# Norm boundaries of an four-layer fp32 kernel: wide products ended bank by bank, two weight splits moved to GpSimd

## What is computed

```python
# first block, twice
hs = hs + rms_norm(mixer(rms_norm(hs, w0)), w1)
hs = hs + rms_norm(conv_ffn(rms_norm(hs, w2)), w3)
# second block, twice
x = layer_norm(ALPHA * x + mixer(x), g_mix, b_mix)
x = layer_norm(ALPHA * x + swiglu(x), g_ffn, b_ffn)
```

## Time and profile before

| | |
|---|---|
| median of 3 runs | 1444.98 us (1444.98 to 1446.88) |
| span of the profiled execution | 1443.1 us |
| PE busy | 1423.5 us, 99% |
| DVE, ACT, Pool busy | 1013.4, 779.4, 294.0 us |
| chain that ended last | PE 81%, DVE 12%, issue 3%, ACT 3% |
| granted PE clock | 0.999 of full over the span |

### The profile page before, as it was taken

One profiled execution on the slowest core, in us unless ns is written; L12 is line 12 of the kernel. 1 busy time (PEld: TensorE's weight loads), 2 busy tenths in 40 slices (PEclk: granted clock), 3 DMA queues, 4 the chain that ended last, 5 costly groups with the idle time before them and its releaser, 6 DMA issues.

```text
span 1443.1 us, 31771 instructions
## 1 busy us (share of the span) xinstructions
PE 1423.5 (99%) x11333; PEld 1363.9 (95%) x11333; DVE 1013.4 (70%) x1701; ACT 779.4 (54%) x1399; POOL 294.0 (20%) x348
## 2 busy tenths in 40 slices
PE   9999999999999999999999999999999999999997
PEld 8999888899999999999999999999999989999986
DVE  7884957659876477569888477587664687776645
ACT  6556324556655366466565356464453567654542
POOL 3804002103444000002544000013330012033310
PEclk9999999999999999999999999999999999999999
DMA  7551231244655535344666544546556433565552
GB/s 256 177 175 47 88 101 47 93 142 160 190 175 175 175 119 189 103 146 128 193 189 189 182 134 152 164 146 200 183 168 204 152 116 118 163 217 186 183 180 91
DMA packets 60996, 223.57 MB, mean 155 GB/s; under 512 B 6768, under 2 KB 6896, under 8 KB 60528
## 3 DMA queue, kind: packets, MB, share of 16 engines
q1 hardware_dynamic: 60624, 220.17, 48.1%
q10 hardware_dynamic: 288, 2.23, 0.4%
HBM read 221.32 MB, written 1.05 MB: 154 GB/s over the span
## 4 chain that ended last, share of the span: by engine, by line
PE 81%; DVE 12%; issue 3%; ACT 3%; DVEq 1%; ACTq 0%; POOL 0%; POOLq 0%
PE bank L440 20%; PE bank L441 20%; PE bank L442 20%; DVE wlo L415 3%; PE bank L461 2%; PE bank L1168 2%; PE bank L462 1%; PE bank L468 1%; DVE bank L947 1%; PE bank L3284 1%; PE bank L3285 1%; PE bank L3287 1%; ACT cv L831 1%; DVE cv L839 1%; DVE work L1782 1%
## 5 line engine op out<-in xcount | busy, mean ns | idle before, releaser
L415 DVE TENSOR_TENSOR wlo<-raw,whi 128x1024 fp32r<-128x1024 f32 x397 | 501.4, 1268 | 249.3 <-ACT whi L410 248.8
L410 ACT ACTIVATE whi<-raw 128x1024 fp32r<-128x1024 f32 x397 | 415.1, 1056 | 288.6 <-PE bank L442 240.6
L440 PE MATMUL bank<-xs,whi 128*128 128x258 f32 (+2 forms) x1984 | 569.2, 287 | 0.0
L441 PE MATMUL bank<-xs,whi 128*128 128x258 f32 (+2 forms) x1984 | 563.9, 284 | 0.0
L442 PE MATMUL bank<-xs,wlo 128*128 128x258 f32 (+2 forms) x1984 | 561.6, 283 | 0.0
L440 PEld LDWEIGHTS bank<-xs,whi 128*128 128x128 f32 x1984 | 374.2, 189 | 3.0 <-issue 1.6
L442 PEld LDWEIGHTS bank<-xs,wlo 128*128 128x128 f32 x1984 | 375.0, 189 | 0.0
L441 PEld LDWEIGHTS bank<-xs,whi 128*128 128x128 f32 x1984 | 374.3, 189 | 0.6 <-issue 0.2
L440 PE MATMUL bank<-hf,whi 128*128 (+3 forms) x848 | 241.3, 285 | 2.0 <-DVE cv L839 0.8
L441 PE MATMUL bank<-hf,whi 128*128 (+3 forms) x848 | 240.3, 283 | 0.0
L442 PE MATMUL bank<-hf,wlo 128*128 (+3 forms) x848 | 240.2, 283 | 0.0
(11 more groups left out here) (516 smaller groups left out, 1671.8 us busy)
## 6 DMA issues: line engine op xcount, KB each, us to landing
raw<-stream SPq DMA_DIRECT2D x412, 512.0 KB, 3.7
con<-consts SPq DMA_DIRECT2D x1, 1284.5 KB, 10.5
big<-mla ACTq DMA_DIRECT2D x1, 1152.0 KB, 7.8
hs_sb<-hs SPq DMA_DIRECT2D x2, 544.0 KB, 4.2
work<-last ACTq DMA_DIRECT2D x1, 1024.0 KB, 9.1
y_out<-work SPq DMA_DIRECT2D x4, 256.0 KB, 2.0
par<-params SPq DMA_DIRECT2D x1, 420.0 KB, 7.9
par<-params SPq DMA_DIRECT2D x1, 224.0 KB, 4.8
```

The lines of the kernel that those rows point to most:

```text
L410: nc.scalar.activation(whi[:, s, :], raw[:, s, :], ACT.Copy).then_inc(hi_split, 1)
L415: nc.vector.tensor_tensor(wlo[:, s, :], raw[:, s, :], whi[:, s, :].bitcast(F32), ALU.subtract).then_inc(block_split, 1)
L440: nc.tensor.matmul(out_, whi[:, slot, w], hi, start=start, stop=False)
L441: nc.tensor.matmul(out_, whi[:, slot, w], lo, start=False, stop=False)
```

## The change

1. `pe_wide`: the last two rows are no longer done one after the other. `last_two` goes through the eight banks and does both rows in each, so that bank m is complete every 6 matmuls; both blocks are used up only at bank 7.
2. Sums: DVE adds the squares of tiles 0 to 6 (`LAST_SUM = 6`; in the layer norms the first seven, `YSUM = 7`), each addition followed by that bank's `scaled`; PE makes two accumulations instead of four (six in the layer norms). All eight banks are now copied into `y`.
3. Splits: `split_lo_pool` gives the low parts of B1 and B2 to Pool. ACT makes B1's high part behind the table load, B2's behind the squares (in the layer norms behind the beta column, before the first `c{m}`). DVE waits for Pool's two before it splits B3. The queue of Pool's other work stands behind these splits.
4. The wave: block B2 starts with its high part alone (`hi_split`), and its low-part matmuls are done from step `LATE = 5` on, five of the eight at the end.
5. DVE's order in the wave: `lo(m-2)` between `y{m}` and `h{m}` (behind `c{m}` in the layer norms) instead of `lo(m-1)` behind them.

```diff
+    def split_lo_pool(pool, phase):
+        for n in (used_after(phase) + 1, used_after(phase) + 2):
+            s = n % SLOTS
+            pool.wait_ge(hi_split, splits(n))
+            pool.wait_ge(block_split, splits(n - 1))
+            nc.gpsimd.tensor_tensor(wlo[:, s, :], raw[:, s, :], whi[:, s, :].bitcast(F32), ALU.subtract).then_inc(block_split, 1)
+        pool.wait_ge(block_split, splits(used_after(phase) + 2))
...
+            if k == LATE:
+                pe.wait_ge(block_split, splits(b0 + AHEAD - 1))
+            for c in range(k - LATE, k - LATE + 1) if k < KC else range(KC - LATE, KC):
+                if c >= 0:
+                    last = mm(rhs_out(g0 + AHEAD - 1, phase), wlo[:, (b0 + AHEAD - 1) % SLOTS, c * P:(c + 1) * P], xs[:, c, T], start=False, stop=(c == KC - 1))
...
+        def last_two():
+            for m in range(8):
+                for k in (n - 2, n - 1):
...
+                    last = three(rhs_out(g0 + m, phase), (b0 + k) % SLOTS, m, hf[:, half[k], T], hf[:, half[n + k], T], False, k == n - 1)
+                    if m == 7:
+                        last.then_inc(block_used, 1)
...
-        sums_pe(pe, name, post_src(name), g, ((5, True, False), (6, False, False), (0, False, False), (7, False, True)), T1, POST_FIRST[name])
+        sums_pe(pe, name, post_src(name), g, ((0, True, False), (7, False, True)), T1, POST_FIRST[name])
...
-        for m in range(1, IN_BANK):
+        for m in range(1, KC):
+            if m <= LAST_SUM:
+                dve.wait_ge(*S("norm", "act").at(f"{name}_{m}"))
+                if m > 1:
+                    dve.wait_ge(*v.at(f"{name}_sum{m - 1}"))
+                nc.vector.tensor_tensor(sq[:, 0, lo:T1], sq[:, 0, lo:T1], sq[:, m, lo:T1], ALU.add).then_inc(*v.mark(f"{name}_sum{m}"))
             scaled(m)
-        split()
...
+        nc.vector.tensor_tensor(y[:, m, t], y[:, m, t], rs[:, 1, t], ALU.mult).then_inc(*v.mark(f"{name}_y{m}"))
+        if m > 1:
+            lo(m - 2)
         dve.wait_ge(*v.at(f"{name}_y{m}"))
...
-    YSUM = 3
+    YSUM = 7
...
-        sums_pe(pe, name + "m", ln_src(name), g, ((0, True, False), (3, False, False), (4, False, False), (5, False, False),
-                                                  (6, False, False), (7, False, True)), T2)
+        sums_pe(pe, name + "m", ln_src(name), g, ((0, True, False), (7, False, True)), T2)
...
-            act.wait_ge(block_used, used_after(PHASE_BEFORE[phase]) - 1)
+            act.wait_ge(block_used, FIRST_BLOCK[PHASE_BEFORE[phase]])
             nc.scalar.activation(xs[:, 0:KC, T2:TB], alone(beta, 2), ACT.Copy).then_inc(*a_.mark(f"{name}_bhi"))
+            split_hi(act, used_after(PHASE_BEFORE[phase]) + AHEAD - 1)
...
         if phase:
+            dve.wait_ge(block_split, splits(fourth(phase) - 1))
             split_lo(dve, fourth(phase))
...
-        split_all(act, split_hi, "down0", 1, COUNT["down0"] - 2)
+        split_all(act, split_hi, "down0", 1, COUNT["down0"] - 3)
         nc.scalar.preload_act_table_set(LN_EXP)
+        split_hi(act, used_after("down0") + 1)
         post_act(act, "post1", G["post1"], "down0")
...
-        split_all(dve, split_lo, "down0", 1, COUNT["down0"] - 2)
-        post_dve(dve, "post1", G["post1"], 3, lambda: split_lo(dve, used_after("down0") + AHEAD - 1))
+        split_all(dve, split_lo, "down0", 1, COUNT["down0"] - 3)
+        post_dve(dve, "post1", G["post1"], 3)
```

More of the change, by code:

```diff
@@ L457, in pe_tiles @@
                     o, s = rhs_out(g0 + j, phase), (b0 + j) % SLOTS
+                    behind_split = j == AHEAD - 1
                     if k == 0:
-                        pe.wait_ge(block_split, splits(b0 + j))
+                        pe.wait_ge(*((hi_split if behind_split else block_split), splits(b0 + j)))
                         pe.wait_ge(bank_free, g0 + j + 1)
                     mm(o, whi[:, s, w], xs[:, k, T], start=(k == 0), stop=False)
-                    mm(o, wlo[:, s, w], xs[:, k, T], start=False, stop=False)
+                    if not behind_split:
+                        mm(o, wlo[:, s, w], xs[:, k, T], start=False, stop=False)
             if k:
@@ L538, in rows @@
                     bank_ready(pe, (g0 + m) % 8)
-                last = three(rhs_out(g0 + m, phase), (b0 + k) % SLOTS, m, hf[:, half[at] if i is None else at, T], hf[:, half[lo] if i is None else lo, T], k == 0, k == n - 1)
-                if i is None and k == n - 1 and m < 7:
-                    last.then_inc(*S("wide", "pe").mark(f"{phase}_m{m}"))
+                last = three(rhs_out(g0 + m, phase), (b0 + k) % SLOTS, m, hf[:, half[at] if i is None else at, T], hf[:, half[lo] if i is None else lo, T], k == 0, False)
             if done:
                 last.then_inc(block_used, 1)
+        def last_two():
+            for m in range(8):
+                for k in (n - 2, n - 1):
+                    if m == 0:
+                        pe.wait_ge(block_split, splits(b0 + k))
+                        ready(pe, k, None)
+                    last = three(rhs_out(g0 + m, phase), (b0 + k) % SLOTS, m, hf[:, half[k], T], hf[:, half[n + k], T], False, k == n - 1)
+                    if m == 7:
+                        last.then_inc(block_used, 1)
+                    elif k == n - 1:
+                        last.then_inc(*S("wide", "pe").mark(f"{phase}_m{m}"))
         if n == 22:
@@ L549, in pe_wide @@
                     rows(k, i)
-            for k in range(17, 22):
+            for k in range(17, 20):
                 rows(k)
+            last_two()
         else:
@@ L558, in pe_wide @@
                         between(pe, k)
-            for k in range(together, n):
+            for k in range(together, n - 2):
                 rows(k)
+            last_two()
     def pe_sum(pe, name, g, src, T):
@@ L706, in post_act, with post_dve @@
         nc.scalar.activation(rs[:, 1, lo:T1], rs[:, 1, lo:T1], ACT.Exp, scale=-0.5).then_inc(*S("norm", "act").mark(f"{name}_scale"))
-    def post_dve(dve, name, g, row, split):
+    def post_dve(dve, name, g, row):
         v, lo = S("norm", "dve"), POST_FIRST[name]
@@ L810, in last_dve @@
         for m in range(KC):
[L811 to L814, removed]
+            add_y(dve, post, m, lo)
+        dve.wait_ge(block_split, splits(fourth("ev_in") - 1))
         split_lo(dve, fourth("ev_in"))
@@ L2341, in ln_act, with ln_dve @@
         act_scale(act, name + "v", g + 1, rs[:, 0, 0:T2], T2, D, eps_ln, meanwhile=lambda: split_hi(act, fifth(phase)) if phase == "od_in" else None)
-    def ln_dve(dve, n, which, layer, phase, wide, split):
+    def ln_dve(dve, n, which, layer, phase, wide):
         name, g = f"ln{n}", G[f"lm{n}"]
@@ L2377, in ln_dve @@
                 nc.vector.memset(w_bias[:, 0:1], 0.0).then_inc(bank_free, 1)
[L2378 to L2382, removed]
+            if phase and m > 1:
+                lo(m - 2)
+            if phase == "od_in" and m in (3, 5, 7):
+                pair_sum(dve, name + "v", m - 2, T2)
+            if phase == "od_in" and m == 6:
                 four_sum(dve, name + "v", 3, T2)
         if phase:
+            lo(KC - 2)
             lo(KC - 1)
```

89 lines of the change are left out of this document (44 added, 45 removed).

## The result

The changed kernel takes **1462.81 us** (median of 4 runs, 1461.40 to 1464.38) against 1445.93 (1444.98 to 1447.55) for the kernel before beside it: 1.0115 times as long, 95% interval 1.0102 to 1.0127, 16.9 us more. The forecast was 1467.3, its range 1451 to 1480. The direction and the cause were right. Two terms of the sum were taken too high, by 6.4 us together, and a small gain on paper was not there.

What follows compares the result with a forecast made beforehand. PE, busy 1423.5 of 1443.1 us, bounds the kernel, leaving seven norm boundaries to decide. Holds 2 x 0.7 + 2 x 3.0 + 3 x 2.8 = 15.8 us, plus clock 6.5, make 22.3 on 1444.98: 1467.3 us, range 1451 to 1480.

Steps and rivals of the forecast that it cites:

- Pool's split: At each boundary: a 1024-element Pool split takes 2.4 us and holds DVE's two-source SBUF operations for about 2.3 us.
- Pool's long operation lets DVE through: Rival at the boundaries: DVE's sums keep 0.43 to 0.45 us during Pool's splits; 1439.8 us in all; chance 0.09.
- Posts with 272 tokens: Boundaries post0 and post1: `sum1` held, `y0` 1.0 us later, wave gains 0.2; taken as 0.7 us lost each.
- Posts with 258 or 256 tokens: Boundaries post2 and post3: Pool asks 0.04 us before `sum6` and holds it; 3.0 us lost each, alternatively 0.7.
- Layer norms: Boundaries ln0 to ln2: Pool's splits hold `ysum1` and `ysum5`, `c0` starts later; 2.8 us lost each.
- The paper gain: All seven boundaries without Pool's hold: sums beside PE and shorter waves save 4 x 0.75 + 3 x 0.7, about 5 us.
- The staggered order: DVE's wave step falls from 1.24 to about 1.12 us; 0.2 us gained per post wave, nothing in layer norms.
- Clock: PE's waits at five boundaries may drop it to 1.2 GHz, 2.6 us each; half of the five counted, 6.5 us.
- Pool loses all races and the clock stays: Rival over all boundaries: four times 0.7 and three times 2.8, 11.2 us more, 1456.2; inside the range given 0.80.
- Pool wins all, and the clock falls each time: Rival over all boundaries: 4 x 3.0 + 8.4 + 7 x 2.6 = 38.6 us more, 1483.6; chance 0.05.
- Waits and queues at nothing: Pool's later work, SP's block loads, late `block_used` and PE's wait for B2's low part: all costed at nothing.

Runs made afterwards that it cites:

- run 5: Changed kernel with each of Pool's two splits made in four operations of 256 elements instead of one of 1024: 1448.32 us, 1.0013 of the kernel before.
- run 4: Changed kernel with more matmuls that nobody reads ahead of PE's sums (15 post, 36 layer norm), to keep PE busy: 1458.04 us, 1.0079 of the kernel before.
- run 9: Changed kernel with `scaled(6)` ahead of `sum6` in the four post boundaries, so `sum6` is asked for later: 1476.82 us, 1.0213 of the kernel before.
- run 1: Changed kernel with both of Pool's splits (B1 and B2) made by DVE instead: 1451.36 us, 1.0024 of the kernel before.
- run 7: Changed kernel with both splits on DVE, one sum (post) or two (layer norm) back on PE, B2's split and late matmuls rearranged: 1439.79 us, 0.9957 of before.
- run 8: Kernel before with only DVE's staggered order added, in the four post waves: 1442.92 us, 0.9977 of the kernel before.
- run 10: The changed kernel again, unaltered, measured beside the exchange of `scaled(6)` and `sum6`: 1466.21 us, 1.0141 of the kernel before.
- run 2: Changed kernel with Pool splitting only B1 and DVE splitting B2: 1456.31 us, 1.0059 of the kernel before.
- run 3: Changed kernel with Pool splitting only B2 and DVE splitting B1: 1456.68 us, 1.0067 of the kernel before.
- run 6: Kernel before with Pool's two splits as the only change, replacing DVE's two: 1453.33 us, 1.0058 of the kernel before.

## Why the prediction was right, and where it was off

**Pool's split: right.** 2.4 us were taken from the line through 256 and 512 elements, with bounds of 2.0 and 2.8; 2.34 to 2.40 us came out where it ran undisturbed. The rule that decided, two-source SBUF operations held until about 0.13 us before Pool's end while operations with a PSUM source pass, was read from rows of 256 and 512 elements and held at 1024 (L2383 at 2.00 and 2.52, L2378 at 0.41). The Trainium skill says in "SBUF — State Buffer", section "SBUF: two separate sides", that the shared port pair is locked for the whole instruction, against a DVE operation with two SBUF inputs too; by this rule, the trace agrees (2.52 us instead of 0.42). The rival "Pool's long operation lets DVE through" is ruled out, and run 5 shows that something near it comes true with pieces of 256. A slip beside it changes nothing: the line through 0.74 and 1.30 us gives 4.7 us for 2048 elements and not 4.8.

**Posts with 272 tokens: right.** `y0` 1.0 us later and 0.7 net each were forecast; `y0` starts at E + 4.03 in post1 instead of 3.03, and run 4 gives 0.67 and 0.60 without the clock.

**Posts with 258 or 256 tokens: the mechanism right, the term mis-sized.** The step that failed is "Pool asks at 649.99, first by 0.04 us". Shifted by the later E (650.23 against 648.55), that made Pool ask at 651.67 and `sum6` at 651.71; both carry 651.68 in the trace. The two requests were right within 0.03 us, but DVE has the port. The term was 2 x 3.0 = 6.0 us and measured 0.70 + 1.03 = 1.7 (run 4). Its other end, 0.7 each, is near that; run 9 shows what losing costs. A margin of 0.04 us is less than the start times were forecast to, as the prediction itself said ("coin tosses"), and the term should have stood between both ends.

**Layer norms: right within 6%.** 3 x 2.8 = 8.4 forecast, 8.9 measured in run 4, with PE idle for 4.43 us where E + 4.3 was forecast. "No margin is small here" was wrong, though: 0.3 us were forecast between Pool's second split and `ysum5`, and Pool was first by 0.15, 0.10 and 0.08 us (1140.79 against 1140.89 in ln1). That the term came out with so little left is partly luck. Run 5 shows the other side of it: without the long hold the same boundaries gain 0.4 to 0.8 us.

**The paper gain: wrong for the posts.** "The sum on paper is 4 x 0.75 + 3 x 0.7, about 5 us less". Run 5 is the nearest to it. Its layer norms gain 0.38, 0.78 and 0.39, where 0.7 each was meant, but its posts lose 0.47, 0.43, 0.40 and 0.77, so that it is 0.5 us over before in all. The step that failed is "DVE could then add `sum1` to `sum6` beside PE": a sum and a copy take DVE 0.76 us and a bank is ready every 0.75, so whatever delays the first sum, a split in run 1 or a piece in run 5, is still there at the end, and PE's first sum starts 0.83 to 1.24 us after E in the posts of both. With one sum back on PE (run 7) that wait is gone and `y0` comes 0.48 us earlier than before. The prediction named the 0.77 against 0.75 where it costed the hold, and forgot it on paper; the rival at 1439.8 thus had too low a time. The staggered order was rightly priced: 0.2 us a wave net of 0.6 for the five late low-part matmuls makes 0.8 by itself, and run 8 gives 0.83. In the changed kernel the late matmuls take 0.4 to 0.6 of that back (waves of 9.94, 9.53 and 9.48 us in post0, post2 and post3 instead of 9.50, 9.13 and 8.90).

**Clock: the kind right, the price too high.** The step that failed is "2.6 us each": half of five falls, 6.5 us, was an estimate; five falls came and cost 4.4, about 0.9 each. By the boundaries' ends against run 4 they cost 0.8 and 0.0 us in post0 and post1 and 1.0, 1.6 and 1.0 in the layer norms. In ln1 the sums do take 0.94 us more, as forecast (2.04 against 1.10), but only some 0.6 more is lost from there to the wave's end. That there were five is luck: the prediction looked for them in post2, post3 and the layer norms, behind waits of over 4 us; post2 and post3 had none, and two came in post0 and post1 behind 1.86 and 1.85 us. At post1 the fall cost nothing. The wave ends at E + 15.51 with it and E + 15.49 without (run 10): it starts 0.54 us later and is 0.5 shorter, and DVE's `y0` starts at the same E + 4.0, so DVE seems to set the end there.

**The forecast as a whole.** It was 22.3 us over before, and 16.9 came out. Of the 5.4 between, 4.3 are the two posts and 2.1 the clock; 0.5 in the layer norms and the rest elsewhere go the other way. The 0.95 us by which the kernel before itself was above 1444.98 make the error in the total 4.5 us. "Pool loses all races and the clock stays", forecast at 11.2 us, is run 4, with 12.1 us of span. "Pool wins all, and the clock falls each time", forecast at 38.6, is run 9, at 1476.82 - 1447.43 = 29.4. Both rivals were real, and the changed kernel lies between them: DVE got the ties, and the clock fell.

**Waits and queues at nothing: right.** 16.25 of 16.5 us are in the seven boundaries. What the prediction left out is a fall of the clock elsewhere, as at 1220.5 in run 10.

**What stays open.** Why DVE gets the port when both requests carry the same time, within 0.03 us, wasn't tried; it did in post2 and post3 of both profiled executions. What decides between a fall of 3.4 and one of 6.8 us is open, and so is what the rest of run 1's loss is made of: its boundaries give 3.0 us, and its span is 6.3 longer, of which 2.6 are the early fall told of below. The bank-by-bank rows were not run without the longer sums, so neither has a price of its own.

## What to carry to other kernels

Before work goes to Pool, ask what DVE does in the same 2 us with two SBUF sources: one long Pool instruction holds it as a whole, so cut it into pieces (four of 0.74 us did it here; no other size was tried), or leave it on DVE in a place where PE has work of its own. Where a sum is moved beside another engine's work, compare the step per tile of both (0.79 against 0.71 us here): in runs 1 and 5 DVE was the slower one, and PE waited for it although it had fewer sums to do. And where two engines' requests lie within a few hundredths of a microsecond, price both orders: 0.4 us of delay cost 10.6 in run 9.

## What the runs showed of the hardware that was not expected

**The clock falls behind shorter waits than the prediction took.** Counting all boundaries of the changed kernel's two profiles and of runs 1, 2, 3, 6 and 9 by PE's idle time before its first sum: up to 1.45 us no fall in 15 boundaries; from 1.84 to 2.01 us a fall in 6 of 15; from 2.33 us on a fall in each of 19. In these profiles an idle time of about 2.0 us went either way, and one of 1 us brought no fall.

**The clock also falls where PE hardly idles.** The windows of 119 to 126 us, in a stretch that the change doesn't touch, of the kernel before and then of run 1:

```profile
119.00:126.00 7.00, 5.95 (x46) 5.42 (x46) 4.48 (x15) 3.83 (x14) 0.15 (x1) 1.00 0.00 0
```

```profile
119.00:126.00 7.00, 7.00 (x32) 6.17 (x33) 3.20 (x12) 1.98 (x8) 0.00 (x0) 0.51 0.00 0
```

In run 1, and in the profiles of runs 2, 5, 7 and 8 too, the clock is at its lower level there for 6.8 us, and post0's E comes at 316.5 to 316.7 instead of 313.9 to 314.1. In runs 3 and 9 it is for 3.4 us, and E comes at 315.8 and 315.9. PE's longest idle time in the 15 us before is 0.57 us; before the fall at 1220.5 in run 10 it is 0.71. What brings these falls is open. One of them is up to 0.2% of the time, as much as some of the effects here, and the profiles of before, after and runs 4, 6 and 10 don't have the early one.
